# Two transformer blocks on one core: row sums of a residual stage on TensorE, a new issue order, and constants computed later

## The reference

```python
def rms_norm(x, gain):
    y = x * lax.rsqrt(jnp.mean(x * x, axis=-1, keepdims=True) + 1e-6)
    return y * gain

# block one
h = rms_norm(x, g_pre_mix) * (1 + sc_m) + sh_m
y = concat(s5_mixer, fourier_mixer, window_attention of h @ w_in) @ w_out
x = x + gt_m * rms_norm(y, g_post_mix)                      # stage 1
h = rms_norm(x, g_pre_ffn) * (1 + sc_f) + sh_f
gate, val = split(dwconv3(h @ w_up))
x = x + gt_f * rms_norm((gelu(gate) * val) @ w_down, g_post_ffn)     # stage 2
# block two
u = rms_norm(x, norm_mix_pre)
proj = u @ w_in_2        # ten slots of 256 features, and 4 x 1024 gate logits
mix = sum_k(sigmoid(gates_k) * (branch_k @ w_branch_k)) @ w_out_2    # LRU, pooling, HGRN, short convolution
x = x + rms_norm(mix, norm_mix_post)                        # stage 4
u = rms_norm(x, norm_mlp_pre)
x = x + rms_norm(square(relu(u @ w_up_2)) @ w_down_2, norm_mlp_post)  # last stage
```

## Time and profile before

| | |
|---|---|
| median of 3 runs | 2954.83 us (2952.43 to 2955.93) |
| the profiled execution | 2954.83 us, span 2953.0 us |
| PE busy | 2787.4 us, 94% |
| PE weight loads, beside it | 2156.2 us, 73% |
| DVE busy | 1286.4 us, 44% |
| ACT busy | 873.9 us, 30% |
| POOL busy | 882.1 us, 30% |
| mean granted clock of TensorE | 0.967 |

### The profile page before, as it was taken

The page is one execution under the profiler, slowest core; times in us unless marked ns, Lnnn a source line. Parts: engine busy times, 40 slices in busy tenths (PEclk is TensorE's granted clock), DMA queues, the critical chain, the costliest instruction groups (busy, mean ns, idle before and its releaser), DMA issues.

```text
span 2953.0 us, 31203 instructions
## 1 busy us (share of the span) xinstructions
PE 2787.4 (94%) x12966; PEld 2156.2 (73%) x12966; DVE 1286.4 (44%) x1604; ACT 873.9 (30%) x1311; POOL 882.1 (30%) x413
## 2 busy tenths in 40 slices
PE   6788889989999999979999999999999999999996
PEld 3656646778888888757777777677677888888885
DVE  6646622766444353565747522321555111111115
ACT  4413553432212121234545221111344111222112
POOL 1422113434333333334211111111245333333324
PEclk8989989999999999989999999999999999999998
DMA  6453246311111111223112221111322111111113
GB/s 230 173 137 102 70 156 221 105 70 56 47 50 50 43 50 50 94 92 109 63 51 100 72 72 54 56 52 54 127 87 107 57 50 47 47 50 50 43 50 136
DMA packets 86430, 245.98 MB, mean 83 GB/s; under 512 B 10769, under 2 KB 25617, under 8 KB 86289
## 3 DMA queue, kind: packets, MB, share of 16 engines
q1 hardware_dynamic: 78256, 219.25, 21.9%
q10 hardware_dynamic: 4608, 14.92, 1.3%
q0 software_dynamic: 3424, 9.81, 0.9%
HBM read 206.87 MB, written 37.07 MB: 83 GB/s over the span
## 4 chain that ended last, share of the span: by engine, by line
PE 82%; DVE 8%; ACT 3%; DMA 2%; issue 2%; POOL 2%; SPq 1%; ACTq 0%; POOLq 0%; DVEq 0%
PE ps L1299 24%; PE ps L1300 23%; PE ps L1301 23%; PE pc L1649 3%; PE pss L1599 1%; PE ps L1516 1%; PE ps L1462 1%; DMA adaw<-in_w_ada 1%; PE ps L1337 1%; POOL whl L2819 1%; DVE y L1667 1%; POOL hid L2819 1%; DVE pad L1667 1%; DVE act L1673 1%; DVE pad L1673 1%
## 5 line engine op out<-in xcount | busy, mean ns | idle before, releaser
L2819 POOL TENSOR_TENSOR whl<-wraw,whl 128x1024 fp32r<-128x1024 f32 (+1 forms) x247 | 638.3, 2586 | 1617.2 <-ACT whl L2379 1617.0
L1299 PE MATMUL ps<-act,whl 128*128 128x512 f32 x2464 | 1000.2, 406 | 48.2 <-DVE act L1667 15.8
L1300 PE MATMUL ps<-act,whl 128*128 128x512 f32 x2464 | 975.4, 396 | 0.0
L1301 PE MATMUL ps<-act,whl 128*128 128x512 f32 x2464 | 974.3, 395 | 0.0
L1299 PEld LDWEIGHTS ps<-act,whl 128*128 128x128 f32 x2464 | 469.6, 191 | 193.9 <-issue 82.2
L1300 PEld LDWEIGHTS ps<-act,whl 128*128 128x128 f32 x2464 | 470.1, 191 | 105.2 <-issue 7.9
L1301 PEld LDWEIGHTS ps<-act,whl 128*128 128x128 f32 x2464 | 470.1, 191 | 104.1
L2379 ACT ACTIVATE whl<-wraw 128x1024 fp32r<-128x1024 f32 (+1 forms) x247 | 256.3, 1039 | 430.0 <-PE ps L1301 391.5
L1299 PE MATMUL ps<-hid,whl 128*128 128x512 f32 x864 | 340.6, 394 | 5.4 <-POOL hid L2819 5.4
L1301 PE MATMUL ps<-hid,whl 128*128 128x512 f32 x864 | 338.2, 391 | 0.0
L1300 PE MATMUL ps<-hid,whl 128*128 128x512 f32 x864 | 338.0, 391 | 0.0
(11 more groups left out here) (315 smaller groups left out, 2411.2 us busy)
## 6 DMA issues: line engine op xcount, KB each, us to landing
wraw<-in_w_in SPq DMA_DIRECT2D x63, 512.0 KB, 3.4
wraw<-in_f1u SPq DMA_DIRECT2D x47, 512.0 KB, 3.2
wraw<-in_f2d SPq DMA_DIRECT2D x36, 512.0 KB, 3.3
wraw<-in_f2u SPq DMA_DIRECT2D x35, 512.0 KB, 3.3
wraw<-in_w_out SPq DMA_DIRECT2D x32, 512.0 KB, 3.3
x<-in_w_ada SPq DMA_DIRECT2D x32, 512.0 KB, 5.5
xs<-y SPq DMA_DIRECT2D x24, 512.0 KB, 6.4
x<-in_xT ACTq DMA_DIRECT2D x16, 512.0 KB, 8.7
```

The source lines that it names most:

```text
L1299: pe.matmul(PSB[g.bank][:, :], hi, src[:, 0, k, c], start=e == 0, stop=False)
L1300: pe.matmul(PSB[g.bank][:, :], hi, src[:, 1, k, c], start=False, stop=False)
L1301: m = pe.matmul(PSB[g.bank][:, :], lo, src[:, 0, k, c], start=False, stop=e == len(ks) - 1)
L2819: return g_.tensor_tensor(out, a, b, op)
```

## The change

`residual` issues `r_sq` of piece j right after its `r_add`, where it was issued one turn later, and asks for its next turn after 1.8 us in second halves and 2.2 us in first halves (before: 2.0 and 3.2). In second halves of stages 1, 2 and 4 `r_sum` moves from DVE to PE: each square buffer is summed over its partitions by `rows_of` into the same PSUM columns, accumulating over j, and `r_rows2` does nothing there. The buffer is then free when PE has read it. `b2_consts` goes; its LRU part runs in `b2_init`, with the clearing of `hs`, after the three tiles. The part for `lb` runs in `hg_init`, after the mask's copy on DVE.

```diff
@@ residual
-        for j in range(9):
-            if j < 8:
-                p.put("r_add", s, half, j)
-            if j:
-                b, free = p.use_sq(s, ("raS", s, half, j - 1))
-                p.put("r_sq", s, half, j - 1, b, free)
-                p.sums.append((s, half, j - 1, b))
-            p.add_sums(lambda entry: entry[2] < j - 1)
-            yield 2.0 if j == 8 else 2.0 if half else 3.2
+        sums = []
+        for j in range(8):
+            p.put("r_add", s, half, j)
...
+            b, free = p.use_sq(s, ("np", "rows2", s, half, j) if half else ("raS", s, j))
+            p.put("r_sq", s, half, j, b, free)
+            if half:
+                sums.append((j, b))
+            else:
+                p.sums.append((s, half, j, b))
+            if j:
+                p.add_sums(lambda entry: entry[2] < j)
+            yield 1.8 if half else 2.2
+            if len(sums) > 1:
+                p.put("r_sum", s, half, *sums.pop(0))
+        if final:
             return
         yield 1.0
         p.add_sums()
-        if not half:
+        if half:
+            p.put("r_sum", s, half, *sums.pop(0))
+        else:
             yield 1.0
         p.put("r_rows2", s, half)
         p.put("r_fac2", s, half)
@@ plan
     p.put("b2_load")
-    p.put("b2_consts")
@@ tensor
+            def r_sum(s, half, j, b):
+                if half:
+                    w.wait_ge(*done("rA", "sq", s, half, j))
+                    rows_of(PSS[:, half, :], sqb[s][b], j == 0, j == 7).then_inc(*mark("np", "rows2", s, half, j))
+
             def r_rows2(s, half):
-                w.wait_ge(*done("raS", s, half, 7))
-                rows_of(PSS[:, half, :], ss[s][:, HALF[half]], True, True).then_inc(*mark("np", "rows2", s, half))
+                if half == 0:
+                    w.wait_ge(*done("raS", s, 7))
+                    rows_of(PSS[:, half, :], ss[s][:, HALF[half]], True, True).then_inc(*mark("np", "rows2", s, half, 7))
@@ vector
             def r_sum(s, half, j, b):
+                if half:
+                    return
...
-            def b2_consts():
+            def b2_init():
...
-                w.wait_ge(*done("b2A", "hlb"))
-                tt(cc[:, 2:4], cc[:, 0:2], cc[:, 0:2], ALU.subtract).then_inc(*mark("b2D", "lb0"))
+                for b in range(2):
+                    w.wait_ge(*done(f"d_xs{b}", 2, 4 + b))
+                v.memset(hs[:, :, :], 0.0).then_inc(*mark("hgD", "hs"))
...
             def hg_init():
...
                 w.wait_ge(*done("d_msk"))
                 v.tensor_copy(msk[:, :, :].rearrange("p l s -> p (l s)"), E[:, :]).then_inc(*mark("hgD", "msk"))
+                w.wait_ge(*done("hgA", "hlb"))
+                tt(cc[:, 2:4], cc[:, 0:2], cc[:, 0:2], ALU.subtract).then_inc(*mark("hgD", "lb0"))
+                w.wait_ge(*done("hgA", "lbe"))
+                link(v.reciprocal(cc[:, 4:6], cc[:, 2:4]))
+                link(tt(cc[:, 2:4], cc[:, 2:4], cc[:, 4:6], ALU.mult))
+                link(tt(cc[:, 6:8], cc[:, 2:4], cc[:, 2:4], ALU.subtract))
+                ts(cc[:, 8:10], cc[:, 6:8], -1.0, ALU.mult, 1.0, ALU.add).then_inc(*mark("hgD", "lb"))
@@ scalar
-            def b2_consts():
+            def b2_init():
                 lam = col("lam", 0, 2)
                 s_ = lambda i: cc[:, 24 + 2 * i:26 + 2 * i]
-                av(cc[:, 0:2], col("hlb", 0, 2), ACT.Copy).then_inc(*mark("b2A", "hlb"))
                 av(s_(1), lam, ACT.Abs).then_inc(*step("b2A"))
                 w.wait_ge(*last("b2A"))
                 av(s_(1), s_(1), ACT.Exp, scale=-1.0).then_inc(*mark("b2A", "e"))
-                w.wait_ge(*done("b2D", "lb0"))
-                av(cc[:, 2:4], cc[:, 2:4], ACT.Exp).then_inc(*mark("b2A", "lbe"))
                 w.wait_ge(*done("b2D", "l1"))
                 av(s_(3), s_(2), ACT.Ln).then_inc(*mark("b2A", "ln"))
+
+            def hg_init():
+                av(cc[:, 0:2], col("hlb", 0, 2), ACT.Copy).then_inc(*mark("hgA", "hlb"))
+                w.wait_ge(*done("hgD", "lb0"))
+                av(cc[:, 2:4], cc[:, 2:4], ACT.Exp).then_inc(*mark("hgA", "lbe"))
```

More of the change, by code:

```diff
@@ L628, in residual @@
         yield 1.2
-        if final:
-            for j in range(8):
-                p.put("r_add", s, half, j)
+        sums = []
+        for j in range(8):
+            p.put("r_add", s, half, j)
+            if final:
                 p.put("r_store", s, half, j)
                 yield 1.4
-            return
-        for j in range(9):
-            if j < 8:
-                p.put("r_add", s, half, j)
-            if j:
-                b, free = p.use_sq(s, ("raS", s, half, j - 1))
-                p.put("r_sq", s, half, j - 1, b, free)
-                p.sums.append((s, half, j - 1, b))
-            p.add_sums(lambda entry: entry[2] < j - 1)
-            yield 2.0 if j == 8 else 2.0 if half else 3.2
+                continue
+            b, free = p.use_sq(s, ("np", "rows2", s, half, j) if half else ("raS", s, j))
[9 more added lines that the diff above has]
+                p.put("r_sum", s, half, *sums.pop(0))
+        if final:
+            return
         yield 1.0
         p.add_sums()
-        if not half:
+        if half:
+            p.put("r_sum", s, half, *sums.pop(0))
+        else:
             yield 1.0
@@ L1654, in tensor @@
                      "att_t": att_t, "att_out": att_out, "fft_w": fft_w, "fft_c": fft_c, "fft_s": fft_s, "fft_mid": fft_mid,
-                     "r_rows": r_rows, "r_bc": r_bc, "r_rows2": r_rows2, "r_bc2": r_bc2, "lru_ri": lru_ri, "pool": pool, "hg_v": hg_v,
+                     "r_rows": r_rows, "r_bc": r_bc, "r_sum": r_sum, "r_rows2": r_rows2, "r_bc2": r_bc2, "lru_ri": lru_ri, "pool": pool, "hg_v": hg_v,
                      "hg_sc": hg_sc, "hg_t": hg_t, "hg_o": hg_o, "hg_st": hg_st, "hg_out": hg_out, "merge": merge}
@@ L2040, in r_sum @@
                 else:
-                    w.wait_ge(*done("raS", s, half, j - 1))
+                    w.wait_ge(*done("raS", s, j - 1))
                     m = tt(ss[s][:, c], ss[s][:, c], sqb[s][b], ALU.add)
-                m.then_inc(*mark("raS", s, half, j))
+                m.then_inc(*mark("raS", s, j))
             def r_fac2(s, half):
@@ L2137, in hg_init, with link @@
             def hg_init():
-                for b in range(2):
-                    w.wait_ge(*done(f"d_xs{b}", 2, 4 + b))
-                v.memset(hs[:, :, :], 0.0).then_inc(*mark("hgD", "hs"))
+                def link(m):
+                    m.then_inc(*step("hgD"))
+                    w.wait_ge(*last("hgD"))
                 w.wait_ge(*done("d_msk"))
                 v.tensor_copy(msk[:, :, :].rearrange("p l s -> p (l s)"), E[:, :]).then_inc(*mark("hgD", "msk"))
+                w.wait_ge(*done("hgA", "hlb"))
[5 more added lines that the diff above has]
+                ts(cc[:, 8:10], cc[:, 6:8], -1.0, ALU.mult, 1.0, ALU.add).then_inc(*mark("hgD", "lb"))
+                w.wait_ge(*last("hgD"))
             def hg_f(tl, k):
@@ L2360, in vector @@
                      "ev": ev,
[L2361 removed]
+                     "f1_init": f1_init, "h1_gate": h1_gate, "h1_val": h1_val, "h2": h2, "b2_init": b2_init,
                      "hg_init": hg_init, "hg_f": hg_f, "hg_lv": hg_lv, "hg_qk": hg_qk, "hg_sc": hg_sc, "hg_e": hg_e, "hg_st": hg_st,
@@ L2663, in r_fac2 @@
             def r_fac2(s, half):
-                w.wait_ge(*done("np", "rows2", s, half))
+                w.wait_ge(*done("np", "rows2", s, half, 7))
                 w.wait_ge(*done("rD", "diag", s, half))
```

10 lines of the change are left out of this document (2 added, 8 removed).

## The result

The changed kernel takes 2990.42 us (median of 4, 2983.91 to 2992.25), where the kernel before took 2954.37 us in the same comparison (2952.43 to 2955.93). The ratio is 1.0118, 95% interval [1.0101, 1.0136]: slower by some 35 us. The forecast was +22.7 us, 2977, with a range that ended at 2986. The direction is right, the size is 12 us short and outside the range.

What follows compares the result with a forecast made beforehand. TensorE was taken as busy nearly throughout, so changes count where it waits or its instruction count changes. Terms 8.1 + 5 + 7.5 - 5 + 7.1 = +22.7 us gave 2977 us; range for 8 in 10: 2959 to 2986.

Steps and rivals of the forecast that it cites:

- Part 1: Second halves of stages 1, 2, 4: seven more PE sets each, less wait and slow matmuls, +2.7 a stage, +8.1 us.
- slow tail: Behind a short PE wait, about 8 matmuls take 0.43 instead of 0.23 us: 1.6 us a second half.
- sets cost nothing: Rival on the second halves: PE idles there anyway, so the row-sum sets are free; 2958 us, chance 7%.
- wait for squares: Rival on the second halves: four of 24 row-sum sets wait 1 to 3 us for ACT's square; +8, 2985 us, 12%.
- Part 2: First halves of stages 1 and 4: DVE and ACT miss the faster pace, apply delays last nadds; +7.5 and +5 us.
- Part 3: First half of stage 2: row sums come 5 to 7 us sooner, diagonal held by 1 us; -5 us (-2 to -9).
- Part 4: Constants' new place: ACT waits for the mask, delaying an evacuation that tile 215 needs; +7.1 us (0 to +10).
- the rival built on it: At the constants' new place, the mask lands before ACT gets to it, so they cost 0; 2970 us, chance 13%.

Runs made afterwards that it cites:

- f5: Changed kernel with r_bc2 and apply of the first halves of stages 1 and 4 put behind the last nadd: 2987.73 us, ratio 1.0104.
- g10: Kernel before with the square directly behind its r_add in first halves of stages 1 and 4, old pace: 2971.21 us, ratio 1.0054.
- f6: Changed kernel with the square's one-turn lag back in all three first halves, r_add still every 4 steps: 2982.85 us, ratio 1.0089.
- f7: Changed kernel with r_add every 5 steps again in the three first halves, square still at once: 2984.98 us, ratio 1.0095.
- e4: Changed kernel with the mask copied after the lb constants on DVE in hg_init: 2984.74 us, ratio 1.0094.
- g11: Kernel before with r_bc2 and apply of the three second halves three planner steps sooner: 2944.01 us, ratio 0.9966.
- e3: Changed kernel with the second halves' sums back on DVE, in the old order and pace: 2977.35 us, ratio 1.0075.
- g9: Kernel before with only the constants moved (b2_init and hg_init as in the change): 2960.43 us, ratio 1.0022.
- f8: Kernel before with the changed first half of stage 2 and new planning of second halves, sums kept on DVE: 2955.28 us, ratio 0.9998.

## Why the prediction was wrong

**Part 1, second halves: right.** 0.89 us a set was measured where 0.90 was taken, and the 2.3 us wait went with its slow tail. Stage 1 shows +2.5 (4.2 - 1.7) against +2.7. In stage 4 the 1.7 us given back is lost again before stage 5 (661.29 against 661.61), so +3.9 stays. The timelines show where. Some 42 us behind r_bc2 TensorE waits 3.35 us for GpSimd in both kernels. In the changed kernel slow matmuls follow, in the kernel before none do, as the windows under "What the runs showed of the hardware" show. The rivals that the sets cost nothing or wait for squares are refuted: no set of a second half shows a wait.

**Part 2, first halves of stages 1 and 4: the step that failed.** The mechanism named there happened: VectorE and ScalarE fall behind, TensorE waits at the row sums, and apply stands in front of the last nadds. Its sizes were wrong at three places (stage 4 first, then stage 1).
- *"The last sum ends 1 to 4 us before the 2195.78 of now ... I take row sums at 2193."* That is 36.8 us into the half (stage 1: 545 is 37.2). Measured: 39.38 and 39.48. Short by 2.5 and 2.3. The sums were to come 2.8 us sooner and came 0.2 sooner, outside the 1 to 4 us as well. The prediction saw that "ACT waits for DVE", and priced it within a hand-made queue that still gained from the faster pace. The runs show that the square at once delays the sums by 1.6 to 2.1 us, and that takes back nearly all that the pace brings.
- *From the row sums to r_bc2* 6.8 us was taken; 7.32 and 8.52 were measured. The set of row sums itself takes 1.86 us there, and the slow matmuls behind the same wait last longer in stage 1 (granted clock 0.65 from 548.40 to 552.40) than in stage 4 (0.93 from 2216.50 to 2219.40). Short by 0.5 and 1.7.
- *The tail behind the next r_rows* was taken as 2.0 us. From r_rows to r_bc it is 8.30 and 8.04 us, where it was 5.00 and 5.62: 3.3 and 2.4. Short by 1.3 and 0.4.

From r_bc2 to r_rows, 14.7 and 16.6 were taken, 14.40 and 16.49 measured. With that, and with the 0.4 and 0.1 us by which the part rounded its sums down, these terms add up to the 4.5 us by which stage 4 exceeds the forecast and the 4.4 of stage 1.

What causes the loss of 9.5 and 11.9 us is shown in part. f5 rules out the place of apply as its root. The square at once makes 7.2 and 9.1 of it alone (g10), the faster pace 6.1 and 5.0 alone (f6), so they overlap, and neither can be called the only root. Both edits also plan TensorE's row sums sooner, by 3 and 8 steps, and no run separates that from them.

**Part 3, stage 2: right in its sum, by other terms**, -4.0 in place of -5. The row sums come 5.9 us sooner, within the 5 to 7 of the hand count. Against that stand the wait of 2.52 us in mid-half, which the part doesn't have, and the diagonal, which the part let be held by 1 us: TensorE waits 3.65 us for it in place of 1.29. The wait for the row sums, to be cut to about 12 us, is 7.0, since TensorE comes later. Here both changes help: the half takes 66.36 us with the faster pace alone (f6), 65.27 with the square at once alone (f7), and 63.23 with both.

**Part 4, the constants: right in size.** With Part 1's stage 2 it was to be 9.8 and is 10.1. That the wait in front of tile 215 was to be 6.8 us and is 6.80 is in part luck: counted from r_bc2, TensorE comes there 1.6 us sooner than the part took and the mask's copy starts 1.2 us sooner, and the two nearly cancel. What failed is its lower bound and the rival built on it: with the mask out of the way, part 4 would not be 0 but some 3.8 us (e4). The part priced one of the four table loads that now stand in front of the evacuation.

**The two rules of the Trainium skill** that the prediction weighed. The clock: after a wait of 2.32 us there were slow matmuls in the kernel before, and after one of 0.23 us there were none, in the changed kernel and again in g11. So a gap of this length can have a price here, where the Trainium skill (TensorE: Matmul & The Clock Gate, section "Why this matters for your kernels") warns of longer ones only. But it doesn't have it each time: e3 has the same wait three times without it, and the kernel before already had a wait of 3.36 us (2286.95) with a granted clock of 1.00 behind it, which the prediction didn't read. The table load takes 1.28 us in every row of e4 above, and the next instruction starts 1.29 to 1.30 us after it; the 2.66 us of the Trainium skill (ScalarE: Activation LUTs, section "What ACT_TABLE_LOAD costs") were not seen.

**The rest** of the miss, 1.8 us, lies in Part 3 (+1.0), stage 4's second half (+1.2), -0.2 in stage 1's and +0.3 at stage 2's second half with the mask, and -0.5 behind hgrn. The range failed since Part 2 gave a lower bound and no upper one, and the upper end of the range came from the rival on waiting sets. Its working held no price for the case that the row sums come no sooner at all.

## What to carry to other kernels

A lag of one turn between two engines that feed each other is not idle time. Before taking it out, write both queues for one full turn and see whether each instruction's input is ready when its engine gets there. And where TensorE waits behind a step, look first at how long that step's own input has been ready. Moving r_bc2 of the second halves by three planner steps brought 10 us, since its input lay ready for 2.9 us. Planning the row sums of stages 1 and 4 sooner only moved TensorE in front of an input that wasn't there.

## What the runs showed of the hardware that was not expected

The same wait is followed by slow matmuls in one trace and by none in another. Windows of 4.00 us, half a microsecond behind a wait of 2.32 us for the activations in stage 4's second half, in g10 and in e3:

```profile
2261.97:2265.97 4.00, 4.00 (x12) 3.09 (x12) 3.92 (x7) 2.53 (x4) 2.50 (x3) 0.57 0.02 4
```

```profile
2271.14:2275.14 4.00, 4.00 (x19) 3.22 (x19) 3.92 (x7) 2.54 (x4) 2.49 (x3) 1.00 0.02 4
```

and behind the wait for GpSimd further on in stage 4, 3.36 us in the kernel before and 3.35 us in the changed one:

```profile
2287.45:2291.45 4.00, 4.00 (x20) 3.25 (x19) 1.90 (x3) 2.01 (x2) 4.00 (x2) 1.00 0.06 15
```

```profile
2316.00:2320.00 4.00, 4.00 (x12) 3.13 (x11) 1.37 (x2) 2.00 (x2) 4.00 (x2) 0.59 0.05 9
```

The four kernels with the wait behind r_bc2 in all three second halves (before, e3, g9 and g10) have it twelve times, at 2.32 to 2.48 us. Eight times the granted clock behind it is 0.57 to 0.70, four times 1.00. Among the shorter ones, 2.02 us (1417.24 in g10) and 1.67 us (1409.56 before) are followed by 1.00, and 1.95 us (1408.76 in f8) by 0.61. What decides it isn't shown. The price, where it falls due, can be read in stage 1: from r_bc2 to TensorE's next wait it is 38.23 us in the kernel before, with the slow matmuls, and 36.66 in e3, without them. That is 1.57 us, near the 1.6 of the prediction. So a stretch can differ between two traces with nothing changed in it: from stage 1 to stage 2 it is 679.77 us in the kernel before and 681.37 in g9.

A set of row sums takes 0.95 us in the stream of the second halves, and 1.86 us right behind the waits of 7.30 us in the changed kernel. Behind a wait of 3.14 us in f6 it took 1.05.
